# The first four modulation blocks of an encoder kernel: other loads, two blocks on VectorE, two as one-column matmuls

## The reference

```python
c_act = jax.nn.silu(c)
for l in range(DEPTH):
    mod = (c_act @ w_ada[l] + b_ada[l])[:, None, :]
    sh_a, sc_a, g_a, sh_m, sc_m, g_m = jnp.split(mod, 6, axis=-1)
    h = x * (1.0 + sc_a) + sh_a
    proj = h @ w_in[l]
    ...                      # three kinds of attention, one output projection
    x = layer_norm(ALPHA * x + (1.0 + g_a) * y, ln1_g[l], ln1_b[l])
    h = x * (1.0 + sc_m) + sh_m
    y = jnp.square(jax.nn.relu(h @ w1[l])) @ w2[l]
    x = layer_norm(ALPHA * x + (1.0 + g_m) * y, ln2_g[l], ln2_b[l])
```

## Time and profile before

| | |
|---|---|
| median of 3 runs | 1546.07 us (1544.27 to 1549.59) |
| profiled execution: span from the first to the last instruction | 1541.4 us |
| PE busy | 1351.1 us, 88% |
| DVE busy | 1092.3 us, 71% |
| ACT, POOL busy | 598.9 us, 284.4 us |
| mean granted clock of TensorE | 0.954 |

### The profile page before, as it was taken

The page is one execution under the profiler, slowest core; times in us unless marked ns, Lnnn a source line. Parts: engine busy times, 40 slices in busy tenths (PEclk is TensorE's granted clock), DMA queues, the critical chain, the costliest instruction groups (busy, mean ns, idle before and its releaser), DMA issues.

```text
span 1541.4 us, 23167 instructions
## 1 busy us (share of the span) xinstructions
PE 1351.1 (88%) x6728; PEld 1129.0 (73%) x6728; DVE 1092.3 (71%) x1830; ACT 598.9 (39%) x1216; POOL 284.4 (18%) x282
## 2 busy tenths in 40 slices
PE   5598987898699999999939999879977999999992
PEld 2597876786588787878739977768766878788772
DVE  6958789877965565565777778989687655654668
ACT  0246488751332222222124547867142322222221
POOL 0513033220700000000460402323052000000024
PEclk9899999899899999999969999989998999999996
DMA  8664600005133333334326462010422333333421
GB/s 304 225 195 150 213 13 13 25 21 171 42 110 124 118 121 105 108 120 150 96 69 196 144 219 86 1 37 1 137 89 89 124 114 97 119 122 122 147 97 55
DMA packets 91843, 173.09 MB, mean 112 GB/s; under 512 B 8092, under 2 KB 18716, under 8 KB 91736
## 3 DMA queue, kind: packets, MB, share of 16 engines
q1 hardware_dynamic: 91208, 169.74, 33.9%
q10 hardware_dynamic: 528, 2.10, 0.4%
HBM read 167.61 MB, written 4.19 MB: 111 GB/s over the span
## 4 chain that ended last, share of the span: by engine, by line
PE 58%; DVE 19%; issue 10%; DMA 6%; ACT 4%; POOL 1%; DVEq 1%; SPq 0%; ACTq 0%; POOLq 0%
PE bank L1286 19%; PE bank L1288 18%; PE bank L1287 18%; DVE hT_hi L855 3%; DMA ada_w<-in_w_ada 2%; DVE smax L1030 2%; DVE pt_lo L1043 1%; DMA slab_raw<-in_w 1%; DMA band<-bias_rows 1%; DVE ada_sum L803 1%; DVE slab_lo L847 1%; DVE X L1071 1%; DVE k_lo L1001 1%; DVE tmp L1068 1%; DVE prob L1023 1%
## 5 line engine op out<-in xcount | busy, mean ns | idle before, releaser
L1286 PE MATMUL bank<-hT_hi,slab_hi 128*128 128x512 f32 x576 | 227.2, 394 | 24.1 <-DVE slab_lo L847 15.1
L1287 PE MATMUL bank<-hT_lo,slab_hi 128*128 128x512 f32 x576 | 226.2, 393 | 0.0
L1288 PE MATMUL bank<-hT_hi,slab_lo 128*128 128x512 f32 x576 | 226.2, 393 | 0.0
L1286 PE MATMUL bank<-slab_hi,h_hi 128*128 128x512 f32 x512 | 203.8, 398 | 6.2 <-ACT mod_a L774 6.2
L1287 PE MATMUL bank<-slab_lo,h_hi 128*128 128x512 f32 x512 | 202.3, 395 | 0.0
L1288 PE MATMUL bank<-slab_hi,h_lo 128*128 128x512 f32 x512 | 202.1, 395 | 0.0
L1286 PE MATMUL bank<-slab_hi,hT_hi 128*128 128x384 f32 (+3 forms) x448 | 154.1, 344 | 37.9 <-DVE slab_lo L847 22.4
L1123 DVE TENSOR_TENSOR slab_lo<-slab_raw,slab_hi 128x512 fp32r<-128x512 f32 x240 | 157.4, 711 | 24.4 <-ACT slab_hi L757 24.3
L803 DVE SCALAR_TENSOR_TENSOR ada_sum<-ada_w,c_col,ada_sum 128x512 f32<-128x512 f32 x196 | 146.8, 749 | 24.2 <-DMA ada_w<-in_w_ada 20.2
L1288 PE MATMUL bank<-slab_hi,hT_lo 128*128 128x384 f32 (+3 forms) x448 | 152.9, 341 | 0.0
L1287 PE MATMUL bank<-slab_lo,hT_hi 128*128 128x384 f32 (+3 forms) x448 | 152.8, 341 | 0.0
(11 more groups left out here) (197 smaller groups left out, 2650.7 us busy)
## 6 DMA issues: line engine op xcount, KB each, us to landing
slab_raw<-in_w SPq DMA_DIRECT2D x256, 256.0 KB, 2.7
ada_w<-in_w_ada SPq DMA_DIRECT2D x56, 1024.0 KB, 5.5
slab_raw<-in_w_in SPq DMA_DIRECT2D x48, 192.0 KB, 3.0
slab_raw<-in_w_o SPq DMA_DIRECT2D x32, 256.0 KB, 2.7
slab_raw<-in_w_in SPq DMA_DIRECT2D x16, 256.0 KB, 4.7
lnrow<-in_ln_rows SPq DMA_DIRECT2D x8, 512.0 KB, 5.7
band<-bias_rows SPq DMA_DIRECT2D x8, 448.0 KB, 3.2
slab_raw<-in_w_in SPq DMA_DIRECT2D x16, 144.0 KB, 3.1
```

The lines of the kernel that those rows point to most:

```text
L1286: pe.matmul(dst, a_hi, w_hi, start=first, stop=False)
L1287: pe.matmul(dst, a_hi, w_lo, start=False, stop=False)
L1288: return pe.matmul(dst, a_lo, w_hi, start=False, stop=last)
```

## The change

The four blocks are loaded whole, with no wait between loads, into a region (ada0, 64 KB in each partition) that is free until the first layer starts; onehot and lncnt are loaded ahead of them, and ropeT and ropeK later, in each layer. The bias b_ada of the four blocks comes as columns (bcol). Blocks 0 and 1 are summed by DVE as before (first_sum), now with a plain product as the start. Blocks 2 and 3 are formed on PE (first_cols): for each half, each of four column groups and each of four k, a 128x128 tile of w_ada is the stationary operand and a column of c_col the moving one. DVE adds the two halves and bcol, and does what ACT did. The four relative-bias rows are issued in another order, POOL fills lnrow only after a wait, and some semaphore counts are adapted.

```diff
--- before.py
+++ after.py
@@ -128,6 +128,7 @@
         mod_m = keep("mod_m", [P, 16])
         aff = keep("aff", [P, 2, 2, KT])
         colpack = keep("colpack", [P, 37])
+        bcol = keep("bcol", [P, 16])
         growrow = keep("growrow", [P, 256])
         ident = keep("ident", [P, P])
         ones = keep("ones", [P, P])
@@ -193,6 +194,7 @@
         relu = over("relu", [P, 2, S], 59392)
         sqr = over("sqr", [P, 2, S], 63488)
 
+        ada0 = over("ada0", [P, 2 * AHEAD, KT // 2, 512], 28672)
         relb = over("relb", [32, 4, P], 0)
         rel = over("rel", [32, 4], 2048)
         onehot = over("onehot", [32, 1024], 4096)
@@ -216,6 +218,8 @@
             sem, ("c_in", "rel_in", "table_in", "const_in", "x_in", "small_in", "up_in", "ln_in", "ropec_in"))
         slab_in = [sem(f"slab_in{i}") for i in range(RING)]
         ada_in = [sem(f"ada_in{i}") for i in range(2)]
+        ada0_in = [sem(f"ada0_in{i}") for i in range(2 * AHEAD)]
+        bcol_in, ada0_sum, ada0_cols, ada0_used = map(sem, ("bcol_in", "ada0_sum", "ada0_cols", "ada0_used"))
         band_in, band_out, stored = sem("band_in"), sem("band_out"), sem("stored")
 
         setup_pool, setup_dve, setup_act, setup_pe = map(sem, ("setup_pool", "setup_dve", "setup_act", "setup_pe"))
@@ -296,19 +300,17 @@
                 if half == 0:
                     sp.dma_start(ada_b[0:1, :], t_in["b_ada"][lay, :, col]).then_inc(ada_in[0], 16)
 
+            sp.dma_start(onehot[:, :], t_in["onehot"]).then_inc(table_in, 16)
+            sp.dma_start(lncnt[:, :], t_in["lncnt"].broadcast_to([P, 1024])).then_inc(table_in, 16)
+            for m in (0, 1, 4, 5, 2, 3, 6, 7):
+                b, half = divmod(m, 2)
+                src = t_in["w_ada"][0, 512 * half:512 * half + 512, 512 * b:512 * b + 512]
+                sp.dma_start(ada0[:, m, :, :], src.rearrange("(k p) n -> p k n", p=P)).then_inc(ada0_in[m], 16)
+                if m == 3:
+                    sp.dma_start(bcol[:, :], t_in["b_ada_col"]).then_inc(bcol_in, 16)
+                    sp.dma_start(X[:, :, :], t_in["x"].rearrange("(t p) d -> p t d", p=P)).then_inc(x_in, 16)
             sp.wait_ge(setup_pool, 1)
-            for n in range(2 * AHEAD):
-                if n >= 2:
-                    sp.wait_ge(ada_half, n - 1)
-                ada_load(0, slice(512 * (n // 2), 512 * (n // 2) + 512), n % 2)
-                if n == 1:
-                    sp.dma_start(onehot[:, :], t_in["onehot"]).then_inc(table_in, 16)
-                    sp.dma_start(lncnt[:, :], t_in["lncnt"].broadcast_to([P, 1024])).then_inc(table_in, 16)
-                if n == 3:
-                    sp.dma_start(X[:, :, :], t_in["x"].rearrange("(t p) d -> p t d", p=P)).then_inc(x_in, 16)
-                if n == 2 * AHEAD - 1:
-                    sp.dma_start(ropeT[:, :, :], t_in["ropeT"]).then_inc(const_in, 16)
-                    sp.dma_start(ropeK[:, :, :, :], t_in["ropeK"]).then_inc(const_in, 16)
+
             def slab(dst_slot, src, at):
                 wait_apart(sp, slab_free, at)
                 sp.dma_start(slab_raw[:, dst_slot, 0:src.shape[-1]], src).then_inc(slab_in[dst_slot], 16)
@@ -322,6 +324,8 @@
                     slab(i % RING, t_in[name][l, k * P:(k + 1) * P, col:col + width], l * SLABS + i + 1)
                     if i == 7:
                         wait_apart(sp, aff_ready, l * 2 + 1)
+                        sp.dma_start(ropeT[:, :, :], t_in["ropeT"]).then_inc(const_in, 16)
+                        sp.dma_start(ropeK[:, :, :, :], t_in["ropeK"]).then_inc(const_in, 16)
                         sp.dma_start(colpack[:, :], t_in["colpack"][l]).then_inc(small_in, 16)
                         sp.dma_start(growrow[:, :], t_in["growrow"][l].broadcast_to([P, 256])).then_inc(small_in, 16)
                         sp.dma_start(ropeC[:, :, :, :], t_in["ropeC"]).then_inc(ropec_in, 16)
@@ -407,6 +411,7 @@
             pool.wait_ge(setup_pool, 3)
             pool.affine_select(out=ident[:, :], in_=ones[:, :], compare_op=ALU.is_equal, fill=0.0, base=0,
                                pattern=[[-1, P]], channel_multiplier=1).then_inc(setup_pool, 1)
+            pool.wait_ge(ada0_used, 1)
             pool.memset(lnrow[:, 0, :], 1.0).then_inc(setup_pool, 1)
             pool.memset(lnrow[:, 1, :], 0.0).then_inc(setup_pool, 1)
             pool.wait_ge(setup_pool, 6)
@@ -485,11 +490,6 @@
 
             act.wait_ge(c_in, 16)
             act.activation(c_col[:, 1, :], c_col[:, 0, :], ACT.Exp, scale=-1.0).then_inc(setup_act, 1)
-            for b in range(AHEAD):
-                act.wait_ge(mod_ready, b + 1)
-                act.activation(mod_a[:, 4 * b:4 * b + 4], bank[b][:, 0:4], ACT.Copy,
-                               bias=float(b >= 2)).then_inc(setup_act, 1)
-
             act.wait_ge(setup_dve, 2 + 4)
             act.dma_start(scratch.rearrange("h p n -> p h n"), frow[:, :, :]).then_inc(band_out, 16)
             act.wait_ge(x_in, 16)
@@ -795,7 +795,7 @@
             dve.wait_ge(dve_step, 2)
             dve.tensor_tensor(c_col[:, 1, :], c_col[:, 0, :], c_col[:, 3, :], ALU.mult).then_inc(setup_dve, 1)
             dve.wait_ge(setup_dve, 1)
-            SETUP_STEPS = 2 + AHEAD * 6
+            SETUP_STEPS = 2 + 2 * (KT - 1) + 2
 
             def ada_piece(k, slot):
 
@@ -806,23 +806,49 @@
 
             dve.wait_ge(rel_in, 16)
             dve.tensor_copy(relb[:, :, :], rel[:, :].unsqueeze(2).broadcast_to([32, 4, P])).then_inc(setup_dve, 1)
-            for blk in range(AHEAD):
+            dve.wait_ge(table_in, 32)
+
+            def bias_row(h):
+                dve.wait_ge(setup_pe, h + 1)
+                dve.tensor_tensor(frow[:, h, 0:512], bank[6][:, :], lncnt[:, 0:512], ALU.add)
+                dve.tensor_tensor(frow[:, h, 512:1024], bank[7][:, :], lncnt[:, 512:1024], ALU.add
+                                  ).then_inc(setup_dve, 1)
+
+            def first_sum(b):
+
+                dst = ada_sum[:, b, :]
                 for k in range(KT):
+                    if k % 4 == 0:
+                        dve.wait_ge(ada0_in[2 * b + k // 4], 16)
+                    w, c = ada0[:, 2 * b + k // 4, k % 4, :], c_col[:, 1, k:k + 1]
                     if k == 0:
-                        dve.wait_ge(ada_in[0], (blk + 1) * 32)
-                    elif k == 4:
-                        dve.wait_ge(ada_in[1], (blk + 1) * 16)
-                        dve.wait_ge(ada_half, 2 * blk + 1)
+                        ins = dve.tensor_scalar(dst, w, c, None, ALU.mult)
                     else:
-                        dve.wait_ge(dve_step, 2 + 6 * blk + k - k // 4)
-                    ada_piece(k, blk).then_inc(ada_half if k % 4 == 3 else dve_step, 1)
-
-                dve.wait_ge(table_in, 32)
-                dve.wait_ge(setup_pe, blk + 1)
-                dve.tensor_tensor(frow[:, blk, 0:512], bank[6][:, :], lncnt[:, 0:512], ALU.add)
-                dve.tensor_tensor(frow[:, blk, 512:1024], bank[7][:, :], lncnt[:, 512:1024], ALU.add
-                                  ).then_inc(setup_dve, 1)
-            dve.wait_ge(setup_act, 1 + AHEAD)
+                        dve.wait_ge(dve_step, 2 + (KT - 1) * b + k)
+                        ins = dve.scalar_tensor_tensor(out=dst, in0=w, scalar=c, in1=dst, op0=ALU.mult, op1=ALU.add)
+                    ins.then_inc(dve_step if k < KT - 1 else ada0_sum, 1)
+
+            bias_row(0)
+            bias_row(1)
+            first_sum(0)
+            bias_row(2)
+            first_sum(1)
+            bias_row(3)
+            dve.wait_ge(bcol_in, 16)
+            for n, b in enumerate((2, 3)):
+                at = slice(4 * b, 4 * b + 4)
+                dve.wait_ge(ada0_cols, n + 1)
+                dve.tensor_tensor(mod_a[:, at], bank[b][:, 0:4], bcol[:, at], ALU.add).then_inc(dve_step, 1)
+                dve.wait_ge(dve_step, 2 + 2 * (KT - 1) + n + 1)
+                dve.scalar_tensor_tensor(out=mod_a[:, at], in0=bank[b][:, 4:8], scalar=1.0, in1=mod_a[:, at],
+                                         op0=ALU.add, op1=ALU.add).then_inc(ada0_used, 1)
+            dve.wait_ge(mod_ready, 2)
+            for b in range(2):
+                at = slice(4 * b, 4 * b + 4)
+                dve.tensor_tensor(mod_a[:, at], bank[b][:, 0:4], bcol[:, at], ALU.add).then_inc(mod_ready, 1)
+            dve.sem_inc(ada_half, 2 * AHEAD)
+            dve.wait_ge(ada0_used, 2)
+            dve.wait_ge(mod_ready, AHEAD)
             dve.tensor_copy(aff[:, 0, 0, :], mod_a[:, 8:16])
             dve.tensor_copy(aff[:, 0, 1, :], mod_a[:, 0:8]).then_inc(aff_ready, 1)
 
@@ -863,7 +889,7 @@
 
                         dve.wait_ge(mod_ready, l * NBLK + AHEAD + max(n - 3, 0))
                     if k % 4 == 0:
-                        dve.wait_ge(ada_in[k // 4], (l * NBLK + AHEAD + n + 1) * (32 if k == 0 else 16))
+                        dve.wait_ge(ada_in[k // 4], (l * NBLK + n + 1) * (32 if k == 0 else 16))
                         dve.wait_ge(ada_half, l * 2 * NBLK + 2 * (AHEAD + n) + k // 4)
```

(41 more changed lines are left out.)

## The result

The changed kernel took 1558.24 us (median of 6 runs, 1556.21 to 1559.62) beside 1545.99 us of the kernel before (6 runs, 1540.72 to 1549.59): a ratio of 1.0076, 95% interval 1.0057 to 1.0094, so 12 us slower. A second set of six runs gave 1557.34 us and 1.0081 (1.0053 to 1.0108).

The account below looks back on a forecast made before the run. PE carries most of the span, but the start stage was judged by its PE-DVE chain: steps sum to 59.6 against 43.81, 15.8 us later. 1546.1 + 15.8 = 1561.9, with small DMA relief 1561.5 us; range 1554 to 1567.

Parts of the forecast that it names:

- tables there, PE starts: Start of the stage: PE waits for onehot and lncnt, landed at 8.0 us, bounds 7.2 to 10.3.
- bias row 0 and its addition: First relative-bias row: 3.85 us from PE to DVE, then DVE's two additions, 1.3 us.
- bias row 1: Second relative-bias row on PE, after row 0's addition because it reuses banks 6 and 7: 3.7 us, to 16.8.
- first_cols(2): Block 2's one-column stream on PE: 64 records of 0.224 us at the lower clock, 14.3 us, to 31.1.
- bias row 2, addition: Third relative-bias row, on PE behind block 2's stream, then DVE's addition: 3.85 + 1.3 us, to 36.3.
- first_sum(1): DVE's sum of block 1, only after bias row 2's addition: 6.3 us, to 42.6.
- mod_cols: PE's one-column matmuls for block 1 after DVE's sum: 1.8 us, to 44.4.
- first_cols(3) and pipeline's end: Block 3's one-column stream, issued last on PE: 14.3 us, to 58.7, plus 0.1 for the pipeline's end.
- tail: End of the stage: pipeline's end, four short DVE operations and PE's start, 0.8 us in all, bounds 0.5 to 1.3.
- the two rivals on the clock: Higher clock in both streams: 7.3 us a block, 1547.8 us, chance 0.06; bias rows too: 1541.2 us, chance 0.04.
- The loads: Rival: the prefetch queue stalls; 5 us more (1566.5) only if the rate fell to some 210 GB/s, chance 0.03.
- The rope tables: ropeT and ropeK loaded in both layers, 0.65 MB ahead of other loads: taken as nought, bounds -3 to +2 us.

Follow-up runs that it names:

- e1: Changed kernel with block 3 summed by VectorE again, block 2 still one-column matmuls on PE; 1555.85 us, ratio 1.006.
- e2: Changed kernel's prefetch with all four blocks summed by VectorE, no one-column blocks, block 0's first half loaded ahead of the tables, X last; 1544.93 us, ratio 0.9997.
- e8: Changed kernel with eight extra f32 matmuls of 512 columns, results unused, ahead of first_cols(2); 1559.5 us in a single run.
- e3: Changed kernel with the same column of c moved 64 times over in first_cols, same weight loads; 1559.33 us, ratio 1.0077.
- e7: As e2, but ropeT and ropeK loaded once before the layers, as in the kernel before; 1546.04 us, ratio 1.0006.
- e10: e2 repeated unchanged; 1543.94 us, ratio 0.9991 against the kernel before.
- e4: Changed kernel with first_cols(3) issued on PE before its wait for first_sum(1); 1556.45 us, ratio 1.0054.

## Why the prediction was right, step by step

It named PE's one-column streams as the new bound, the order of the stage, and the clock level at which they would run. e1 and e2 show that the streams are the cause: with one gone the first transpose comes 6.4 us earlier, with both 17.7. Times in us:

| step | predicted | measured |
|---|---|---|
| tables there, PE starts | 8.0 | 6.72 |
| bias row 0 and its addition | 5.1 | 5.20 (to 11.92) |
| bias row 1 | 3.7 | 3.71 (to 15.63) |
| first_cols(2) | 14.3 | 13.74 (to 29.37) |
| bias row 2, addition | 5.1 | 5.02 (to 34.39) |
| first_sum(1) | 6.3 | 6.10 (to 40.49) |
| mod_cols | 1.8 | 1.73 (to 42.22) |
| first_cols(3) and pipeline's end | 14.4 | 13.83 (to 56.05) |
| tail | 0.7 | 0.81 |
| first transpose | 59.6 | 56.86 |

The steps as rounded here add up to 59.4; the prediction carried them unrounded to 59.6. The 2.7 us that the sum was too late come from three terms. The table load took 4.5 us from issue to landing (the broadcasts of the earlier trace rows had 4.9 to 6.5): PE started 1.3 us sooner, at 6.72, below the lower bound of 7.2. A record of the streams cost 215 ns, not the 224 of mod_cols, perhaps because a run of only eight has the cost of its start in it, which no run separates: 1.1 us over both. And the plain product takes 0.48 us where the product with addition takes 0.75; the prediction had priced both alike: 0.2 us. DVE stood idle for 10.19 and 14.15 us where 10 and 15 were expected.

The clock at the start was read rightly from the pace. The windows print 1.00 for the whole of the first 60 us of the changed kernel, and that alone does not tell the level: in the kernel before, the records of the first X transposes start 0.21 us apart from 44 to 48 us and 0.11 apart from 49 on, at a printed 1.00 on both sides. e8 has the pace beside a fall that the windows show: one-column records start 0.11 us apart at 1.00 and 0.21 apart at 0.50, and the latter is the pace of the changed kernel's streams. Of the two rivals on the clock neither came: the streams ran low throughout, and so did the four bias rows (3.7 us for four records of 512 columns, some 0.9 each, where those of e8's eight took 0.85 before the rise and 0.43 after it). That a run of matmuls is unbroken did not raise the clock by itself. In e8 it rose some 4 us into the eight dense f32 matmuls, of 512 columns and 128 rows; it stayed at the lower level through streams of 13.8 us with one moving column (the changed kernel) and of 13.9 us with 64 (e3). What in the eight raised it, no run separates.

The loads decided nothing, as argued. The rope tables cost nothing that e7 can tell. The rest of the changed kernel took 1498.8 us where it took 1497.6, and the median's 12.2 us lie within a microsecond of the 13.05 of the first transpose. That agreement is in part luck: the stretch behind the first transpose differs by up to 9 us from version to version, as the experiments showed.

One thing the prediction took for granted was wrong, though it did not cost it here: that a microsecond at the first transpose is a microsecond of the time. For e2, e7 and e10, 4.0 to 4.6 us in the start brought between a gain of 0.9 us and a loss of 0.1. Its figure of 4.7 us between the span and the median of the kernel before also mixes two things: a time is some 1.6 us longer than the span of the same execution (1557.25 and 1555.7 for the changed kernel), and the rest is that the profiled execution was a quick one.

## What to carry to other kernels

Before work moves from a vector sum to the tensor engine as matmuls of one column, price it by records at the clock level that the engine has there: here 64 records of 215 ns, each with its weight load, 13.8 us, replaced a vector sum of 6.1 us. The one other order that was tried (e4) hid no more than 2 us, since the engine had become the one that bound the stage. When two engines hand work back and forth, walk through both streams in program order and look who waits. The prefetch in the same change was sound, and became a gain of 8 us once the one-column blocks and the additions of the bias rows were both off the path. A few microseconds won at the start are not yet won in the time: compare the later parts one by one, with the busy time of the bounding engine in each, before an average such as the mean clock is taken for the cause.

## What the runs showed of the hardware

An f32 matmul with 64 moving columns took as long as one with a single column (13.92 and 13.81 us for 64 records, two to a matmul). In e8 TensorE's clock rose from its lower level during eight dense f32 matmuls, 8.9 us in all (their records 0.85 us apart from 16.91 to 19.47, 0.43 from 20.07 on), and it fell at about 30 us, to a granted 0.50, within the one-column stream that had begun at 24.79. The code behind the first transpose, the same in all versions but for the place of the rope loads, took 1497.6 to 1506.9 us in the eleven profiles of the table, at mean granted clocks of 0.954 to 0.945. A DVE cast of 128x512 took 0.43 us alone and 2.6 us beside POOL's product of 128x1024.
